# Up-projections of four feed-forward layers: the seven partial products of a slab are added inside the banks, ScalarE scales the outer taps of the convolution, and 22 more slabs are multiplied by seven products

## The reference, cut to what matters

```python
def conv_ffn(h, w_up, conv_w, conv_b, w_down):      # h: 256 x 1024
    a = h @ w_up                                      # 1024 x 5632
    pad = jnp.pad(a, ((0, 0), (CONV_W - 1, 0), (0, 0)))
    y = conv_b
    for j in range(CONV_W):                           # 3 taps over the tokens
        y = y + conv_w[j] * pad[:, j:j + S, :]
    gate, val = jnp.split(y, 2, axis=-1)
    return (jax.nn.silu(gate) * val) @ w_down         # 2816 x 1024
```

## Time and profile before

| | |
|---|---|
| median of 3 runs | 2782.33 us (2777.73 to 2786.01) |
| the profiled execution, its own time | 2779.76 us |
| its span in the trace | 2777.9 us |
| TensorE busy | 2710.6 us (98%) |
| VectorE busy | 1516.8 us (55%) |
| ScalarE busy | 440.9 us (16%) |
| GpSimd busy | 93.9 us (3%) |

### The profile page before, as it was taken

How to read it: one execution, slowest core, us unless ns; L and a number is a source line. 1 busy time by engine, 2 the same in 40 slices (tenths; PEclk the granted TensorE clock), 3 DMA queues, 4 the chain that set the end, 5 groups by cost and what they waited for, 6 DMA issues and landing times.

```text
span 2777.9 us, 52049 instructions
## 1 busy us (share of the span) xinstructions
PE 2710.6 (98%) x22508; PEld 2147.4 (77%) x22508; DVE 1516.8 (55%) x3437; ACT 440.9 (16%) x899; POOL 93.9 (3%) x180
## 2 busy tenths in 40 slices
PE   7999999999999999999999999999999999999987
PEld 6889997899998999999998899988435335742634
DVE  4558867898677887686866658756410111011011
ACT  3112205221132220211211300021100000100001
POOL 0110001100001000000000000000000000000000
PEclk9999999999999999999999999999999999999999
DMA  9777555775536766564444444455999999999996
GB/s 364 284 269 253 205 209 213 274 244 192 203 113 240 259 221 233 216 216 165 161 165 159 138 162 171 160 204 232 409 427 426 412 427 426 426 427 428 425 428 273
DMA packets 97519, 754.48 MB, mean 272 GB/s; under 512 B 10496, under 2 KB 12048, under 8 KB 42128
## 3 DMA queue, kind: packets, MB, share of 16 engines
q1 hardware_dynamic: 71920, 658.90, 61.1%
q0 software_dynamic: 25344, 92.29, 9.1%
q10 hardware_dynamic: 32, 0.02, 0.0%
HBM read 750.09 MB, written 1.06 MB: 270 GB/s over the span
## 4 chain that ended last, share of the span: by engine, by line
PE 86%; DMA 8%; DVE 4%; ACT 1%; issue 0%; SPq 0%; DVEq 0%; ACTq 0%
PE ps L838 25%; PE ps L741 14%; PE ps L1511 14%; PE ps L1548 7%; PE ps L878 3%; PE ps L1258 3%; PE ps L771 3%; DMA UW<-w_moe_up 2%; PE ps L1373 2%; PE ps L818 2%; PE ps L1178 2%; PE ps L751 2%; PE ps L992 2%; DMA B<-w_moe_down 1%; DMA B<-w_moe_up 1%; DMA A<-w_moe_up 1%
## 5 line engine op out<-in xcount | busy, mean ns | idle before, releaser
L741 PE MATMUL ps<-HT,ring 128*128 128x256 f32 x1856 | 408.5, 379 | 0.0
L741 PEld LDWEIGHTS ps<-HT,ring 128*128 128x128 f32 x1856 | 349.6, 190 | 46.7 <-issue 1.0
L3119 DVE TENSOR_TENSOR C<-C,ps 128x256 f32<-128x256 f32 (+1 forms) x80 | 30.8, 388 | 362.5 <-ACT C L1999 362.5
L838 PE MATMUL ps<-A,UW 128*128 128x128 f32 x1488 | 176.5, 275 | 0.5 <-DVE UW L2116 0.4
L838 PEld LDWEIGHTS ps<-A,UW 128*128 128x128 f32 x1488 | 171.1, 192 | 0.8 <-DVE UW L2116 0.8
L838 PE MATMUL ps<-A,ring 128*128 128x128 f32 x1252 | 158.2, 275 | 0.0
L838 PEld LDWEIGHTS ps<-A,ring 128*128 128x128 f32 x1252 | 149.3, 192 | 0.3
L1258 PE MATMUL ps<-HT,ring 128*128 128x256 f32 x640 | 142.5, 380 | 0.0
L3143 DVE TENSOR_TENSOR X<-X,ps 128x512 f32<-128x512 f32 x24 | 16.5, 688 | 217.7 <-PE ps L1470 217.0
L1258 PEld LDWEIGHTS ps<-HT,ring 128*128 128x128 f32 x640 | 120.3, 190 | 16.9 <-issue 1.2
L838 PE MATMUL ps<-HT,ring 128*128 128x128 f32 x992 | 120.8, 275 | 0.0
(11 more groups left out here) (565 smaller groups left out, 4587.3 us busy)
## 6 DMA issues: line engine op xcount, KB each, us to landing
ring<-w_ff_up SPq DMA_DIRECT2D x88, 1024.0 KB, 4.9
B<-w_moe_up SPq DMA_DIRECT2D x27, 2048.0 KB, 20.8
ring<-w_moe_up SPq DMA_DIRECT2D x26, 2048.0 KB, 20.5
B<-w_ada POOLq DMA_DIRECT2D x72, 512.0 KB, 5.2
ring<-w_ff_down SPq DMA_DIRECT2D x36, 1024.0 KB, 4.8
first_slot<-w_ada POOLq DMA_DIRECT2D x72, 512.0 KB, 5.9
HT<-w_moe_up SPq DMA_DIRECT2D x16, 2048.0 KB, 22.1
ring<-w_moe_down SPq DMA_DIRECT2D x16, 2048.0 KB, 23.4
```

The source lines that it names most:

```text
L741: last = mm(bank[:, j * n:(j + 1) * n], ring[:, slot, k * 256 + j * P:k * 256 + j * P + P], src[:, k, :], start=(k == 0), stop=(k == KD - 1))
L838: last = mm(bank[:, at * P:(at + 1) * P], b if by_token else a, a if by_token else b, start=(n in (0, 2) and k == 0), stop=(n in (6, 5) an ...
```

## The change

In the four `ff_up` sections only (the SwiGLU block keeps its way), a seven slab's products are added inside the banks. TensorE makes a first product into bank x, ScalarE copies it out to SBUF, and then TensorE goes on adding another product onto the same place. There are four copies per slab, of 128x128, and three waits of TensorE for them (`part_done` and `part_copied` are the new semaphores). One product goes to a third bank, ps7, in every slab. VectorE then needs two operations of 128x256 (`up_folded`) in place of six. The banks go round by three pairs and not by four.

In the convolution ScalarE now makes the two outer taps too, scaled, into tiles `scaled` (four more activations of 128x256 for a slab, plain or seven), and VectorE only adds them, for both halves at once: two operations of 128x2x255 and 128x2x254 in place of four.

The order of both engines' loops moves by a step: the centre and the taps of slab m-1 and the Silu and product of slab m-2 now stand in iteration m. Two more iterations follow the last slab. The value differences of the down-projection's first parts stand in iterations 9 and 17, before in 8 and 16.

`UP_SEVENS` gets 14 slabs in each of layers 0 to 2 (3 to 20 without m = 6, 10, 14, 18), and all 19 from 3 to 21 in layer 3: 22 more. The down-projection's three groups use other pairs of banks.

```diff
-UP_SEVENS = {("sw_up", 0): range(3, KF), ("ff_up", DEPTH - 1): [m for m in range(3, 18) if m % 4 != 2]}
+UP_SEVENS = {("sw_up", 0): range(3, KF), ("ff_up", DEPTH - 1): range(3, KF)}
 for layer in range(DEPTH - 1):
-    UP_SEVENS["ff_up", layer] = range(3, 20, 2)
+    UP_SEVENS["ff_up", layer] = [m for m in range(3, 21) if m % 4 != 2]
+FOLD_PAIRS = [(2, 3), (4, 5), (0, 1)]
+FOLD_THIRD = 7
+FOLD_DOWN = [(6, 7), (4, 5), (0, 1)]
...
+        folded = [T[:, 2 * n:2 * n + 2, :].rearrange("p a t -> p (a t)") for n in range(2)]
+        scaled = [T[:, 4 + 2 * n:6 + 2 * n, :] for n in range(2)]
...
+            def sevens_folded(g, banks, sums, values, summed, wait_values):
...
+                product(x, 0, w, 0, lambda k: values[:, k, 0, 0, :], True).then_inc(part_done.tick(), 1)
+                if wait_values:
+                    values_summed.wait(pe)
+                weights_summed.wait(pe)
+                product(y, 1, sums, 2, lambda k: summed(2, k), True).then_inc(part_done.tick(), 1)
+                product(z, 0, sums, 3, lambda k: values[:, k, 1, 1, :], True).then_inc(part_done.tick(), 1)
+                part_copied.wait(pe)
+                product(x, 0, sums, 1, lambda k: summed(1, k)).then_inc(part_done.tick(), 1)
+                part_copied.wait(pe)
+                product(y, 1, w, 3, lambda k: summed(3, k))
+                product(y, 0, w, 1, lambda k: values[:, k, 1, 0, :])
+                part_copied.wait(pe)
+                product(x, 0, sums, 0, lambda k: summed(0, k)).then_inc(slab_done, 1)
+
+            def gemm_up_folded(i):
...
+                    if t > 2:
+                        pe.wait_ge(free_dve, before[sec]["dve"] + max(frees[m] for m in {3: (0,), 4: (0, 1)}.get(t, (t - 3,))))
...
+                def copies(m):
+
+                    (x, y), to = [ps[b] for b in fold_banks(m)], folded[m % 2]
+                    part_done.wait(act)
+                    af(to[:, 0:P], x[:, 0:P], ACT.Copy).then_inc(part_copied.tick(), 1)
+                    part_done.wait(act)
+                    af(to[:, 3 * P:4 * P], y[:, P:2 * P], ACT.Copy).then_inc(part_copied.tick(), 1)
+                    part_done.wait(act)
+                    af(to[:, 2 * P:3 * P], ps[FOLD_THIRD][:, 0:P], ACT.Copy)
+                    part_done.wait(act)
+                    af(to[:, P:2 * P], x[:, 0:P], ACT.Copy).then_inc(part_copied.tick(), 1)
...
+                        for d in (1, 2):
+                            ins = af(scaled[d - 1][:, half, :], src[:, half * TOK:(half + 1) * TOK], ACT.Copy,
+                                     scale=vec[:, c + 2 - d:c + 3 - d])
...
+                for m in range(KF + 2):
+                    if m in UP_SEVENS[sec]:
+                        copies(m)
+                    if m >= 2:
+                        silu(m - 2)
+                    if 1 <= m <= KF:
+                        centre(m - 1)
...
+            def up_folded(i, m, out):
+
+                (x, y), add = [ps[b] for b in fold_banks(m)], folded[m % 2]
+                dve.wait_ge(slab_done, first_slab["ff_up", i] + m + 1)
+                tt(halves(out)[:, :, 0:P], halves(add[:, 0:TOK]), halves(y[:, 0:TOK]), ALU.add)
+                tt(halves(out)[:, :, P:TOK], halves(add[:, TOK:2 * TOK]),
+                   x[:, 0:P].rearrange("p (o t) -> p o t", o=1).to_broadcast([P, 2, P]), ALU.add).then_inc(free_dve, 1)
...
                     for d in (1, 2):
-                        for half in range(2):
-                            c = COL["ff_conv"] + i * KF * 8 + m * 8 + half * 4
-                            o = C[:, m % 4, half, d:TOK]
-                            ins = stt(out=o, in0=src[:, half * TOK:(half + 1) * TOK - d],
-                                      scalar=vec[:, c + 2 - d:c + 3 - d], in1=o, op0=ALU.mult, op1=ALU.add)
+                        o = C[:, m % 4, :, d:TOK]
+                        ins = tt(o, o, scaled[d - 1][:, :, 0:TOK - d], ALU.add)
...
-                for m in range(KF):
+                for m in range(KF + 2):
                     if m in UP_SEVENS[sec]:
-                        up_together(sec, m, up_out[m % 2][:, 0:TOK], up_out[m % 2][:, TOK:2 * TOK])
+                        up_folded(i, m, up_out[m % 2])
                     up_value_sums(sec, m)
                     up_weight_sums(sec, m + 2)
-                    taps(m)
-                    if m:
-                        product(m - 1)
+                    if 1 <= m <= KF:
+                        taps(m - 1)
+                    if m >= 2:
+                        product(m - 2)
                     if m == KF - 2:
                         weight_sums(("ff_down", i), 0)
                     if i + 1 < DEPTH and 0 < m < KF - 1:
                         ada_next(n + m - 1)
-                    if m in (8, 16):
+                    if m in (9, 17):
                         value_sums(m // 8 - 1, made)
```

More of the change, by code:

```diff
@@ L201, in up_banks, with fold_banks, fold_frees @@
     return UP_PAIRS[(m - 2) % 4] if m > 1 else (m, None)
+def fold_banks(m):
+    return FOLD_PAIRS[(m - 2) % 3] if m > 1 else (m, None)
+def fold_frees(layer):
+    order = []
+    for m in range(KF + 1):
+        if m in UP_SEVENS["ff_up", layer]:
+            order.append(m)
+        if m and m - 1 not in UP_SEVENS["ff_up", layer]:
+            order.append(m - 1)
+    return {m: n + 1 for n, m in enumerate(order)}
 def gm_banks(j, m):
@@ L840, in sevens, with product @@
                 last.then_inc(slab_done, 1)
+            def sevens_folded(g, banks, sums, values, summed, wait_values):
+                (x, y), z, w = [ps[b] for b in banks], ps[FOLD_THIRD], seven_w(g)
+                def product(bank, at, stationary, kind, moving, start=False):
+                    for k in range(KD // 2):
+                        last = mm(bank[:, at * P:(at + 1) * P], stationary[:, kind, k, :], moving(k),
+                                  start=(start and k == 0), stop=(k == KD // 2 - 1), skip_group_check=not start)
+                    return last
+                product(x, 0, w, 0, lambda k: values[:, k, 0, 0, :], True).then_inc(part_done.tick(), 1)
[11 more added lines that the diff above has]
+                product(x, 0, sums, 0, lambda k: summed(0, k)).then_inc(slab_done, 1)
@@ new lines, in gemm_up_folded @@
+            def gemm_up_folded(i):
+                sec = ("ff_up", i)
+                g0, frees = first_slab[sec], fold_frees(i)
+                for t in range(1, KF):
+                    g, bank = g0 + t, ps[fold_banks(t)[0]]
+                    slab_wait(g)
+                    if t > 2:
+                        pe.wait_ge(free_dve, before[sec]["dve"] + max(frees[m] for m in {3: (0,), 4: (0, 1)}.get(t, (t - 3,))))
+                    if t in UP_SEVENS[sec]:
+                        sevens_folded(g, fold_banks(t), up_s[t % 2], H4, lambda n, k: up_t[:, n, k, :], t == UP_SEVENS[sec][0])
+                    elif t == 1:
+                        pair_as_made(bank, g % RING).then_inc(slab_done, 1)
+                    else:
+                        pair(bank, g % RING, H).then_inc(slab_done, 1)
@@ L842, in gemm_seven @@
             def gemm_seven(sec, part_wait):
                 g0 = first_slab[sec]
+                pairs = FOLD_DOWN if sec[0] == "ff_down" else UP_PAIRS
                 for m in range(3):
-                    pe.wait_ge(free_dve, before[sec]["dve"] + (m - 3))
+                    pe.wait_ge(free_dve, before[sec]["dve"] + (0 if m and sec[0] == "ff_down" else m - 3))
                     for part, (lo, hi) in enumerate(PAIR_PARTS):
@@ L851, in gemm_seven @@
                             part_wait(lo, hi)
-                        sevens(g, UP_PAIRS[m], seven_s[(3 * m + part) % 2], A4, lambda n, k: seven_t[:, n, k, :], lo, hi, PAIRS, m == 0)
+                        sevens(g, pairs[m], seven_s[(3 * m + part) % 2], A4, lambda n, k: seven_t[:, n, k, :], lo, hi, PAIRS, m == 0)
             def gemm_up(sec):
@@ L1701, in ffn, with centre @@
                 f0 = before[sec]["dve"]
-                for m in range(KF):
-                    seven = m in UP_SEVENS[sec]
-                    if seven:
-                        put_together.wait(act)
+                frees = fold_frees(i)
+                def copies(m):
[8 more added lines that the diff above has]
+                    af(to[:, P:2 * P], x[:, 0:P], ACT.Copy).then_inc(part_copied.tick(), 1)
+                def centre(m):
+                    if m in UP_SEVENS[sec]:
+                        act.wait_ge(free_dve, f0 + frees[m])
                         src = up_out[m % 2]
```

29 lines of the change are left out of this document (16 added, 13 removed).

## The result

The changed kernel takes 2789.78 us (median of 8 runs, 2783.57 to 2792.77), the kernel before 2780.11 us on the same chip (8 runs, 2777.73 to 2786.01). The two medians lie 9.7 us apart, or 0.35%. The ratio that weighs all runs is 1.0029, with a 95% interval from 1.0021 to 1.0038: 8.1 us more, or 0.29%. The forecast was 6.2 us more, which the interval (5.8 to 10.6 us) still takes in. By the ratio the change is just within the bound of 0.3%, by the medians just outside, and the interval says either way that the kernel became a little slower.

What follows compares the result with a forecast made beforehand. TensorE, busy for 98% of the span, was taken as the bound. Gain, entry, value differences and exit: -14.3 + 2.6 + 7.0 + 10.9 = +6.2 us, so 2782.3 + 6.2 = 2788.5 us; 8-in-10 range 2774 to 2798.

Steps and rivals of the forecast that it cites:

- The gain, 14.3 us: Up-projections: 22 plain slabs turned into seven slabs save TensorE 0.652 us each, 14.3 us, if nothing comes late.
- Nothing late in the steady run: Up-projection between the breaks: ScalarE's first copy is always there before TensorE's fourth product, at no cost.
- margin of 0.45 us: Steady run, worst phase: TensorE could go on at 8.48 us and wants to at 8.93.
- Entry: Each layer's slab 3: starts 0.25 us late, its fourth product 0.39 late; 0.64 us, 2.6 us in four layers.
- Value differences: After iterations 9 and 17: late fourth products, 1.60 us a layer in layers 0 to 2, twice 1.12 in layer 3; 7.0 us.
- Exit: Down-projection's second slab: TensorE waits for weight differences, 2.42 us a layer, 3.96 in layer 3; 10.9 us after subtracting 0.07 each.
- New operations: VectorE's new taps priced at 0.69 us each, 1.42 for two; ScalarE's scaled activations spaced 0.42 from SBUF, 0.36 from PSUM.
- The signals at nothing: Seven slabs: the three further signals per slab were taken to cost TensorE nothing.
- each copy or signal costs TensorE a little: Rival, 7%: in seven slabs even a signal or wait met in time holds the next weight load; 2794.6 us.
- all waits are hidden: Rival, 13%: no wait shows anywhere, VectorE leaving the exit 2.4 us earlier; the kernel is 14 us faster, 2768.
- ScalarE as the pace-maker: Rival, 26%: iterations 0.45 us longer make the first copy late in nearly every seven slab; 2793 to 2798, at most 2801.

Runs made afterwards that it cites:

- the waits mended: The changed kernel with down-projection weight differences earlier, slab 0's taps first in iteration 1, and value differences in iterations 12 and 19 (layers 0 to 2): 2768.91 us.
- later value differences: The changed kernel with the value differences of layers 0 to 2 in iterations 12 and 19 in place of 9 and 17: 2786.76 us, ratio 1.0024.
- taps first: The changed kernel with the taps of slab 0 ahead of the value and weight differences in iteration 1: 2786.38 us, ratio 1.0019.
- exit mended in layer 3: The changed kernel with the down-projection's second-slab weight differences ahead of the last slab's taps in layer 3 alone: 2781.41 us, ratio 1.0006.

## Why the prediction was nearly right, step by step

- **The gain, 14.3 us:** right. Seven slabs in the steady run take 6.257 us for 6.253, and with the waits mended the kernel is 10.6 us (ratio) to 12.3 us (medians) faster than before, with late groups of 2.0 us in layer 3 still in it.
- **Nothing late in the steady run:** right, by a priced margin of 0.45 us. No slab but those named is late. The margin's size was not tried by itself.
- **Entry, 0.64 us a layer:** measured 0.54 (slab 3 starts 0.23 us late for 0.25, its fourth product costs 0.31 for 0.39).
- **Value differences, 0.64 + 0.32 + 0.64 in layers 0 to 2, twice 1.12 in layer 3:** the slabs are the right ones, and the sizes are 0.47 + 0.20 + 0.47 and twice 0.98. In sum 5.4 us for 7.0. ScalarE was a little quicker than priced: six activations out of PSUM take 2.32 us (325.73 to 328.05) for the 2.40 of the forecast. (Its own spacings, 2 x 0.46 and 4 x 0.36, add up to 2.36.)
- **Exit, 2.42 us a layer and 3.96 in layer 3, less 0.07:** measured 2.25 and 3.79, before the 0.07 is taken off. In sum 10.3 us for 10.9.
- **New operations:** taps 0.69 us each as taken, the scaled activation 0.493 from SBUF and 0.479 from PSUM, and both overlap as the earlier trace rows had it.
- **The signals at nothing:** right, by the run with 351 more of them. The rival that each copy or signal costs TensorE a little is out with it: a seven slab with all its copies and waits is 0.004 us longer, so 61 of them cost 0.2 us.
- **What was missing from the sum:** the granted clock. My prices for a wait were its length and 0.10 to 0.15 us for the restart. After the 3.5 us wait of layer 3 the same group took 1.5 us more in the profiled execution. After waits of 2 us it took 1.6 more in two layers each of two other kernels that have the same waits. The waits were over-sized by 2.7 us (20.5 for 17.8). What the late groups leave unexplained is some 4.6 us by the ratio, 6.2 by the medians; of this the profiled execution shows 1.5 as the clock at the exit, and the rest is put down to the clock by the mean clocks of the runs, not by rows. The two errors have opposite signs, so the forecast of +6.2 for +8.1 owes part of its accuracy to luck.
- **The rivals:** that all waits are hidden needed an exit earlier by 2.4 us, and VectorE came at the forecast time. ScalarE as the pace-maker would make nearly every fourth product late; of the 61 only 15 have the group of 1.16 us that tells of it, slabs 3, 12, 13 and 20 in layers 0 to 2 and slabs 3, 12 and 20 in layer 3, the ones forecast. The clock as a mechanism stood among none of my rivals, though the trace of before could have shown it. The earlier trace rows gives the clock only in 40 slices, all of which read 9, and the earlier trace rows is a wait of 0.36 us. The rows at 452.67 and 455.00 us above are of that trace: behind a wait of 2.02 us the clock is at 0.50. They could have put a second price on four exit waits of 2.4 us and more.

That an exit wait of 2 us can be followed by the lower clock is shown, in the profiled executions of two kernels that share these waits with the changed kernel. In the changed kernel's own profiled execution the three waits of 2 us were not followed by it. Which of its eight runs lost the clock where is inferred: the three fastest have mean clocks of 0.996, the others 0.992 to 0.995. Why one wait of 2 us is followed by the lower clock and the next is not stays open: in layers 0 and 1 of the kernel with later value differences the wait, the code and the group are the same.

## What to carry to other kernels

When a change moves one engine's order by a step, walk the places where the pattern breaks (entry, a double load, exit) and not only the steady run: here the steady run was free, and late groups of 17.8 us at three breaks took back more than all of the 14.3. Work that a later stage waits for belongs ahead of the last dependent hop, as soon as a buffer for it is free; that one edit turned a loss of 8 us into a gain of 6. And a wait of two microseconds or more on TensorE can have two prices, its length and the clock behind it. Here the longest wait was the one that always had both, so mend the longest first. Before a forecast, look in the trace of before for what the clock does behind the waits that are already there.

## What the runs showed of the hardware

- After waits of 3.4 to 3.5 us the next 24 matmuls of 128 columns took 4.31 to 5.49 us for 2.94, in all seven such waits of four profiled executions, with a granted clock of 0.50 in the windows shown. The Trainium skill (TensorE: Matmul & The Clock Gate, Part 1: The HAM clock gate) has an idle TensorE at half its clock, 1.2 GHz for 2.4. The traces agree with it in the two levels, 0.50 and 1.00.
- After exit waits of 1.98 to 1.99 us the group took 4.57 us in four of twelve profiled cases (layers 1 and 2 of the kernels with later value differences and with taps first) and 2.94 us in the other eight (layer 0 of both, layers 0 to 2 of after and of exit mended in layer 3). After a wait of 2.0 us that all ten kernels have near 453 us, the clock was at 0.50 in seven and at 1.00 in three. After the four waits of 0.9 us it stayed at 1.00.
- The granted clock also stood at 0.50 for 3 to 14 us near 1950 us in all ten profiled executions, in the same code, so the time of a single execution carries some microseconds of chance.
- A wait met late by 0.10 us cost TensorE 0.20 (slab 13 of layer 0), and the list of waits prints nothing for it: the group behind it is 0.10 us longer (1.16 for 1.06).
- An increment by a matmul in mid-slab costs nothing that 351 of them could show (ratio 1.0000, up to 1.0009; a slab still 6.25 us).
